# Projection matmuls whose moving columns alternate between the two 256-column halves of a weight row

## Chip, cores and metric

The kernel runs on one core of a Trainium2 chip. The metric is device time in microseconds (us) of one execution. The kernel before takes 1576.56 us, the median of three runs (1575.62 to 1576.97).

## What is computed

One block of a streaming encoder over 256 tokens of width 2048, all in float32:

```
h      = rms_norm(x, g_mix)
proj   = h @ w_in                      # retention q,k,v,gate; attention q,k,v
ret    = silu(gate) * group_norm(retention(q, k, v))
att    = sliding_window_attention_with_sinks(q, k, v)
merged = sigmoid(h @ w_gate_r) * (ret @ w_ret) + sigmoid(h @ w_gate_a) * (att @ w_att)
x      = x + merged @ w_out
x      = x + square(relu(rms_norm(x, g_ffn) @ w_up)) @ w_down      # width 8192
out    = rms_norm(x, g_fin)
```

## The kernel before

**Blocks.** All products with a weight matrix ("projections") are cut into 69 blocks of 2048 weight rows by 512 columns. A block is 16 chunks `k` of 128 rows, two chunks making a unit `u`. Two token tiles `t` of 128 tokens each have a PSUM accumulator of one bank, 512 float32 columns, so one block fills `acc[parity]`, a tile of 128 x 2 x 512; two of these alternate from block to block.

**Three products for one.** Weights come by DMA as float32 into `raw`. ScalarE copies each unit into `whi` as fp32r (the reduced form in which TensorE multiplies in one pass), VectorE subtracts to get the rest, `wlo`; of the activations there are such pairs too (`ta_hi`, `ta_lo`; `tb_`, `tc_`). A projection is hi x hi + hi x lo + lo x hi. So each chunk and token tile takes three matmuls (line 413): the stationary operand is 128 x 128 of the activations, which gives tokens as the output's partitions, and the moving operand is the chunk's 512 weight columns, neighbours in SBUF. The weight split (ScalarE, line 648; VectorE, line 967) uses a ring of eight chunks, and so is paced by the matmuls that release its slots. From block 37 on (the MLP), a quarter of each block's low parts, `low`, comes through a copy on ScalarE (line 656) and an accumulating DMA (line 1402) instead.

**Exceptions.** The first unit of the first block is done with plain float32 operands (line 469), which the program issues as two instructions per product. The last block does one token tile after the other (line 626, `gemm_by_tile`), so that the first tile's end work lies under the second tile's matmuls.

**Order.** The order is written out by hand and kept by semaphores. Stage 1 projects attention q and retention q, k alternately and mixes attention's small matmuls in between (`tail_a`, `tail_r`); stage 2 does attention's gate and branch; stage 3 retention's v and gate, with the retention itself; stage 4 retention's gate and branch and the merging; stage 5 the output projection (four blocks); stage 6 the MLP in four rounds of four `w_up` and four `w_down` blocks.

**Who reads the accumulators.** ScalarE: `scaled` (line 662) for most blocks, and lines 768 and 771, which sort the columns of the first block, keys and values of four heads. VectorE: `rotate` (lines 1094 to 1097, four products with cosines and sines over both token tiles), `gated_attention` (line 1187), the gating in `tail3` (line 1222), `merge` (line 1274), `add_residual` (line 1303), and line 1384 for the last block. A block's accumulator is needed again only by the second block after it. The readers of accumulators stand among the weight splits in the in-order queues of the two engines.

Of the kernel before, what the change touches and what calls it, by code (L numbers as in the profile page):

```python
# [29 lines left out]
P = 128  # L30
D = 2048
S = 256
TILES = S // P
COLS = 512
# [13 lines left out]
ATT_D = 64  # L48
# [75 lines left out]
ACT_COLS, DVE_COLS = 768, 640  # L124
WARM_UP = 10

OWN_STAGE1, OWN_STAGE2, OWN_STAGE3, OWN_STAGE4 = 18, 1, 1, 1

def build(nc, x, x_t, w_in, w_ret, w_att, w_gate, w_out, w_up, w_down, g_fin,  # L130
# [3 lines left out]
    ds = bass.ds  # L134

    ctx = ExitStack()
    with ctx:
# [139 lines left out]
        gained = buf[2][:, 1, :].rearrange("p (k n) -> p k n", n=S)  # L277
        gmix_at = slice(SMALL - 4 * KCH, SMALL - 3 * KCH)

        block = ctx.enter_context(nc.Block())  # L280

# [109 lines left out]
        def _(pe):  # L392
            def gemm(B, hi, lo, u0, u1):

                for u in range(u0, u1):
                    if u == 0 and B.reused:
                        pe.wait_ge(evacuated[B.parity], B.turn)
                    halves = B.very_first and u == 1
                    by_dma = B.ffn and u >= DVE_UNITS
                    if by_dma:  # L400
                        pe.wait_ge(low_full, B.before * 16 + 32)
                        pe.wait_ge(hi_ready, B.part(u))
                    elif not halves:
                        pe.wait_ge(lo_ready, B.low(u))
                    for kk in range(UCH):
                        if halves:
                            pe.wait_ge(half_lo, kk + 1)
                        k, slot = u * UCH + kk, (u * UCH + kk) % (KCH // 2)
                        low = low4[:, k - DVE_UNITS * UCH, :] if by_dma else wlo[:, slot, :]
                        for t in range(TILES):  # L410
                            tok = slice(t * P, (t + 1) * P)
                            for n, (a, b) in enumerate(((hi, whi[:, slot, :]), (hi, low), (lo, whi[:, slot, :]))):
                                last = nc.tensor.matmul(acc[B.parity][:, t, :], a[:, k, tok], b,  # L413
                                                        start=(k == 0 and n == 0), stop=(k == KCH - 1 and n == 2))
                    last.then_inc(unit_done, 1)

# [48 lines left out]
            for k in range(UCH):  # L465
                pe.wait_ge((first_full, second_full)[k], 16)
                pe.wait_ge(xt_gained, k + 1)
                for t in range(TILES):
                    last = nc.tensor.matmul(acc[0][:, t, :], gained[:, k, t * P:(t + 1) * P], raw[:, k, :],
                                            start=(k == 0), stop=False)  # L470
            last.then_inc(unit_done, 1)
            for u in range(1, UNITS):
# [141 lines left out]
            def gemm_by_tile(B):  # L614

                pe.wait_ge(evacuated[B.parity], B.turn)
                for t in range(TILES):
                    tok = slice(t * P, (t + 1) * P)
                    for u in range(UNITS):
                        if t == 0:  # L620
                            pe.wait_ge(lo_ready, B.low(u))
                        for kk in range(UCH):
                            k = u * UCH + kk
                            whi_k, wlo_k = [last_slot(part, u)[:, kk, :] for part in range(2)]
                            for n, (a, b) in enumerate(((tb_hi, whi_k), (tb_hi, wlo_k), (tb_lo, whi_k))):
                                done = nc.tensor.matmul(acc[B.parity][:, t, :], a[:, k, tok], b,
                                                        start=(k == 0 and n == 0), stop=(k == KCH - 1 and n == 2))
                    done.then_inc(tile_done, 1)

# [7 lines left out]
        def _(act):  # L637
# [20 lines left out]
            def scaled(B, dst, func, scale):  # L658

                act.wait_ge(unit_done, B.unit(UNITS - 1))  # L660
                for t in range(TILES):
                    last = nc.scalar.activation(dst[:, t, :], acc[B.parity][:, t, :], func, scale=scale[:, t:t + 1])
                return last

            def hi_from_turned(turn, dst, g):
# [84 lines left out]
            def stage1(j, first):  # L750
                A, R = Block(B1, 2, j), Block(B1 + 1, 2, j)
                if first:
# [9 lines left out]
                    act.wait_ge(unit_done, Block(0).unit(UNITS - 1))  # L762
                    kd = buf[1][:].rearrange("p t (g e d) -> p t g e d", e=2, d=ATT_D)
                    vd = vwin[:].rearrange("p w g (e d) -> p w g e d", e=2)
                    kv = [acc[0][:, t, :].rearrange("p (s g d) -> p s g d", s=2, d=ATT_D) for t in range(TILES)]
                    twice = [(t, e) for t in range(TILES) for e in range(2)]
                    for t, e in twice:
                        last = nc.scalar.activation(kd[:, t, :, e, :], kv[t][:, 0], ACT.Copy, scale=rstd[:, t:t + 1])
# [189 lines left out]
        def _(dve):  # L958
# [125 lines left out]
            def rotate(g, B):  # L1084

                dve.wait_ge(unit_done, B.unit(UNITS - 1))
                half = RET_QK // 2
                v = acc[B.parity][:].rearrange("p t (h x d) -> p t h x d", x=2, d=half)
                cos = roper[:, 0].unsqueeze(2).to_broadcast([P, TILES, 4, half])
                sin = roper[:, 1].unsqueeze(2).to_broadcast([P, TILES, 4, half])  # L1090
                o = buf[1][:].rearrange("p t (h x d) -> p t h x d", x=2, d=half)
                tmp = [b[:].rearrange("p t (h d) -> p t h d", d=half)[:, :, 4 * i:4 * i + 4, :]
                       for b in (buf[2], buf[3]) for i in range(2)]
                V_.tensor_tensor(tmp[0], v[:, :, :, 0, :], cos, ALU.mult)
                V_.tensor_tensor(tmp[1], v[:, :, :, 1, :], sin, ALU.mult)
                mine.step(V_.tensor_tensor(tmp[2], v[:, :, :, 1, :], cos, ALU.mult))
                V_.tensor_tensor(tmp[3], v[:, :, :, 0, :], sin, ALU.mult).then_inc(evacuated[B.parity], 1)
                dve.wait_ge(turned_1, g + T_Q)
                dve.wait_ge(evacuated[B.parity], B.turn + 1)
                V_.tensor_tensor(o[:, :, :, 0, :], tmp[0], tmp[1], ALU.subtract)  # L1100
                V_.tensor_tensor(o[:, :, :, 1, :], tmp[2], tmp[3], ALU.add).then_inc(rope_ready, 1)
# [80 lines left out]
            def gated_attention(j):  # L1182
# [1 line left out]
                B = Block(B2 + 1, 2, j)  # L1184
                dve.wait_ge(unit_done, B.unit(UNITS - 1))
                mine.wait(dve)
                V_.tensor_tensor(mix[:, :, ds(j * COLS, COLS)], buf[2][:], acc[0][:], ALU.mult).then_inc(evacuated[0], 1)

            tail_a(3, Block(B2), Block(B2 - 1))
            tail_r(3, Block(B2 + 1))  # L1190
# [15 lines left out]
            def tail3(j, B):  # L1206
# [12 lines left out]

                dve.wait_ge(rgate_ready, j + 1)  # L1220
                dve.wait_ge(ret_read, j + 1)
                V_.tensor_tensor(buf[3][:], buf[1][:], acc[0][:], ALU.mult).then_inc(evacuated[0], 1)
                dve.wait_ge(evacuated[0], Block(B3 + 1, 2, j).turn + 1)
                V_.scalar_tensor_tensor(buf[3][:].rearrange(flat), buf[2][:].rearrange(flat), 1.0,
                                        buf[3][:].rearrange(flat), ALU.add, ALU.mult).then_inc(gated_ready, 1)
# [42 lines left out]
            def merge(j):  # L1268
# [2 lines left out]
                dve.wait_ge(unit_done, B.unit(UNITS - 1))  # L1271
                mine.wait(dve)
                dve.wait_ge(t_full, j + T_STAGE4)
                V_.tensor_tensor(buf[3][:], buf[2][:], acc[0][:], ALU.mult).then_inc(evacuated[0], 1)
                dve.wait_ge(evacuated[0], B.turn + 1)
                V_.tensor_tensor(buf[3][:], buf[3][:], mix[:, :, ds(j * COLS, COLS)], ALU.add).then_inc(m_ready, 1)

# [22 lines left out]
            def add_residual(B, j):  # L1300
                dve.wait_ge(unit_done, B.unit(UNITS - 1))
                sl = mix[:, :, j * COLS:(j + 1) * COLS]
                V_.tensor_tensor(sl, sl, acc[B.parity][:], ALU.add).then_inc(evacuated[B.parity], 1)

            def inverse_rms(done):
                mine.step(V_.tensor_reduce(sum2[:], ssq2[:], AX.X, ALU.add))
# [74 lines left out]
            for t in range(TILES):  # L1381
                sl = mix[:, t, early:D]
                dve.wait_ge(tile_done, t + 1)
                V_.tensor_tensor(sl, sl, acc[0][:, t, :], ALU.add).then_inc(added, 1)
                dve.wait_ge(added, t + 1)
                V_.tensor_tensor(final[:, t, early:D], sl, gfin[:, early:D], ALU.mult).then_inc(final_g, 1)
                dve.wait_ge(last_sq, t + 1)
# [89 lines left out]
```

## Time and profile before

| | before |
|---|---|
| median of three runs | 1576.56 us |
| the profiled execution | 1575.47 us |
| its span, first to last instruction | 1573.5 us |
| TensorE matmul busy | 1562.0 us, 99% |
| TensorE weight load busy | 1280.2 us, 81% |
| VectorE busy | 1023.7 us, 65% |
| ScalarE busy | 795.1 us, 51% |
| DMA, mean | 212 GB/s |
| granted TensorE clock, mean | 0.999 of full |

Busy time counts each instruction from start to modelled end, and matmuls overlap: one that lasts 389 ns is followed by the next after some 227 ns. The rate of the stream is therefore read from start times, or from the chain of waits, which gives a stretch of the array's work with its count.

### The profile page before, as it was taken

How to read it: one execution, taken by the hardware profiler on the slowest of the kernel's cores; microseconds unless marked ns; L12 is line 12 of the kernel's file. 1: busy time of each engine (PE TensorE's matmuls, PEld its weight loads, DVE VectorE, ACT ScalarE, POOL GpSimd, SP SyncE). 2: the span in 40 equal slices, each digit the busy share in tenths (PEclk: the TensorE clock that was granted, in tenths of full speed). 3: DMA queues.
4: the chain of work that ended last, by engine and by line, in shares of the span. 5: the costliest groups of instructions: out<-in, count | busy, mean ns of one | idle time of the engine just before them, and what ended most of it. 6: DMA issues, size and time to landing. Idle time of an engine off the chain costs nothing.

```text
span 1573.5 us, 18925 instructions
## 1 busy us (share of the span) xinstructions
PE 1562.0 (99%) x7008; PEld 1280.2 (81%) x7008; DVE 1023.7 (65%) x1344; ACT 795.1 (51%) x1023; POOL 39.4 (3%) x52
## 2 busy tenths in 40 slices
PE   9999999999999999999999999999999999999998
PEld 7777777888888888888878888888888888888886
DVE  5977876544456777666689877347753576437744
ACT  6555555443444444444444555555554555555553
POOL 0000000000000000000000000000000000000000
PEclk9999999999999999999999999999999999999999
DMA  9644554556655565565565877888778887888873
GB/s 362 206 144 152 183 160 161 187 187 222 208 171 175 188 201 168 180 206 192 203 231 181 260 237 237 253 230 254 233 236 251 240 249 218 252 240 241 249 222 117
DMA packets 154392, 333.93 MB, mean 212 GB/s; under 512 B 5600, under 2 KB 5728, under 8 KB 149856
## 3 DMA queue, kind: packets, MB, share of 16 engines
q1 hardware_dynamic: 149296, 299.61, 56.3%
q0 software_dynamic: 4464, 32.51, 10.9%
q10 hardware_dynamic: 576, 1.06, 0.2%
q8 instruction: 36, 0.59, 0.2%
q14 instruction: 20, 0.16, 0.0%
HBM read 298.55 MB, written 2.10 MB: 191 GB/s over the span
## 4 chain that ended last, share of the span: by engine, by line
PE 92%; DVE 4%; DMA 2%; issue 1%; ACT 1%; SPq 0%; POOL 0%; POOLq 0%; DVEq 0%
PE acc L413 89%; DMA raw<-in_w_in 2%; DVE wlo L967 1%; DVE buf L976 1%; PE tps L428 1%; PE pps L455 1%; PE pps L438 0%; DVE kT L976 0%; DVE qT L976 0%; PE sps L446 0%; DVE ta_lo L1366 0%; ACT whi L648 0%; PE tps L557 0%; PE tps L556 0%; PE tps L558 0%
## 5 line engine op out<-in xcount | busy, mean ns | idle before, releaser
L648 ACT ACTIVATE whi<-raw 128x1024 fp32r<-128x1024 f32 x542 | 572.4, 1059 | 662.3 <-PE acc L413 658.2
L967 DVE TENSOR_TENSOR wlo<-raw,whi 128x1024 fp32r<-128x1024 f32 x480 | 586.0, 1226 | 460.9 <-ACT whi L648 457.7
L413 PE MATMUL acc<-whi,ta_hi 128*128 128x512 f32 x1308 | 514.4, 393 | 0.8 <-DVE ta_lo L1010 0.4
L413 PE MATMUL acc<-whi,ta_lo 128*128 128x512 f32 x1308 | 509.5, 390 | 0.0
L413 PE MATMUL acc<-wlo,ta_hi 128*128 128x512 f32 x1180 | 459.2, 389 | 0.0
L413 PEld LDWEIGHTS acc<-whi,ta_hi 128*128 128x128 f32 x1308 | 245.5, 188 | 57.9 <-issue 4.2
L413 PEld LDWEIGHTS acc<-whi,ta_lo 128*128 128x128 f32 x1308 | 245.5, 188 | 51.8
L413 PE MATMUL acc<-whi,tb_hi 128*128 128x512 f32 x736 | 286.7, 389 | 0.0
L413 PE MATMUL acc<-whi,tb_lo 128*128 128x512 f32 x736 | 286.3, 389 | 0.0
L413 PEld LDWEIGHTS acc<-wlo,ta_hi 128*128 128x128 f32 x1180 | 221.6, 188 | 44.8
L413 PE MATMUL acc<-wlo,tb_hi 128*128 128x512 f32 x616 | 239.6, 389 | 0.0
L976 DVE STREAM_TRANSPOSE buf<-buf 32x256 f32<-32x256 f32 x384 | 167.4, 436 | 6.8
L413 PEld LDWEIGHTS acc<-whi,tb_hi 128*128 128x128 f32 x736 | 138.2, 188 | 29.3 <-issue 0.8
L413 PEld LDWEIGHTS acc<-whi,tb_lo 128*128 128x128 f32 x736 | 138.2, 188 | 28.8
L413 PEld LDWEIGHTS acc<-wlo,tb_hi 128*128 128x128 f32 x616 | 115.6, 188 | 23.8
L656 ACT ACTIVATE low<-raw 128x2048 fp32r<-128x2048 f32 x31 | 59.1, 1906 | 0.0
L413 PE MATMUL acc<-whi,tc_hi 128*128 128x512 f32 x128 | 50.0, 390 | 0.9 <-DVE wlo L967 0.9
L413 PE MATMUL acc<-whi,tc_lo 128*128 128x512 f32 x128 | 49.8, 389 | 0.0
L413 PE MATMUL acc<-low,ta_hi 128*128 128x512 f32 x128 | 49.8, 389 | 0.0
L413 PE MATMUL acc<-wlo,tc_hi 128*128 128x512 f32 x128 | 49.8, 389 | 0.0
L1402 POOL DMA_DIRECT2D low<-raw x31 | 27.0, 870 | 889.8 <-ACT low L656 889.8
L413 PE MATMUL acc<-low,tb_hi 128*128 128x512 f32 x120 | 46.7, 389 | 0.0
(139 smaller groups left out, 789.4 us busy)
## 6 DMA issues: line engine op xcount, KB each, us to landing
raw<-in_w_in SPq DMA_DIRECT2D x66, 1024.0 KB, 5.2
raw<-in_w_up SPq DMA_DIRECT2D x64, 1024.0 KB, 5.5
raw<-in_w_down SPq DMA_DIRECT2D x64, 1024.0 KB, 5.2
raw<-in_w_gate SPq DMA_DIRECT2D x32, 1024.0 KB, 5.3
low<-raw POOLq DMA_DIRECT2D x31, 1024.0 KB, 8.1
raw<-in_w_att SPq DMA_DIRECT2D x16, 1024.0 KB, 5.0
raw<-in_w_ret SPq DMA_DIRECT2D x16, 1024.0 KB, 5.0
raw<-in_w_out SPq DMA_DIRECT2D x16, 1024.0 KB, 5.1
```

The lines of the kernel that those rows point to most:

```text
L413: last = nc.tensor.matmul(acc[B.parity][:, t, :], a[:, k, tok], b, start=(k == 0 and n == 0), stop=(k == KCH - 1 and n == 2))
L428: last = nc.tensor.matmul(score[:, h, m, 0:kn], qT[part, c, 2 * m:2 * m + 2, :].rearrange("p a n -> p (a n)"), keys[part, k0:k0 + kn], sta ...
L455: last = nc.tensor.matmul(pps[part, 2 * h:2 * h + 2, :].rearrange(flat), vst[:, KEYS[c][2], part], probT[:, 2 * h:2 * h + 2, :].rearrange( ...
L648: nc.scalar.activation(whi[:, s:s + UCH, :], raw[:, u * UCH:(u + 1) * UCH, :], ACT.Copy).then_inc(hi_ready, 1)
L656: nc.scalar.activation(low4[:], raw[:, DVE_UNITS * UCH:KCH, :], ACT.Copy, scale=-1.0).then_inc(low_set, 1)
L967: V_.tensor_tensor(wlo[:, s:s + UCH, :], raw[:, u * UCH:(u + 1) * UCH, :], whi[:, s:s + UCH, :].bitcast(f32), ALU.subtract).then_inc(lo_re ...
L976: last = V_.transpose(dst(i, o), src[i:i + SQ, :, :, o:o + SQ])
L1402: pool.dma_start(low4[:].bitcast(f32), raw[:, DVE_UNITS * UCH:KCH, :], accum_op=ALU.add).then_inc(low_full, 16)
```

## The change

In SBUF nothing moves. A matmul's moving operand, 512 neighbouring columns, is read through a view that gives column 0, 256, 1, 257, ..., 255, 511. The output is written to neighbouring addresses of the bank, so bank position 2n holds column n, and position 2n+1 column 256+n. All readers of the accumulators read with a step of two elements to get the old order back; what they write lies as before. This holds for lines 413, 469 and 626 alike. Matmuls of attention and retention, the transposes, weight loads and DMAs are as they were.

`rotate` is cut by token tile, since its view would have a dimension too many: eight multiplications over 128 x 256 elements stand for four over 128 x 512, and one counted step on VectorE's own semaphore goes away (OWN_STAGE1 is 17 for 18). The counting of all other semaphores stays.

```diff
-OWN_STAGE1, OWN_STAGE2, OWN_STAGE3, OWN_STAGE4 = 18, 1, 1, 1
+OWN_STAGE1, OWN_STAGE2, OWN_STAGE3, OWN_STAGE4 = 17, 1, 1, 1
...
+        def halves_in_turn(cols):
+            return cols.rearrange("p (b n) -> p n b", b=2)
+        def paired(bank):
+            return bank.rearrange("p (n b) -> p n b", b=2)
+        def unpaired(bank):
+            return bank.rearrange("p (n b) -> p b n", b=2)
+        def unpaired_tiles(banks):
+            return banks.rearrange("p t (n b) -> p t b n", b=2)
+        def by_half(cols):
+            return cols.rearrange("p (b n) -> p b n", b=2)
+        def by_half_tiles(cols):
+            return cols.rearrange("p t (b n) -> p t b n", b=2)
...
-                                last = nc.tensor.matmul(acc[B.parity][:, t, :], a[:, k, tok], b,
+                                last = nc.tensor.matmul(paired(acc[B.parity][:, t, :]), a[:, k, tok], halves_in_turn(b),
...
-                    last = nc.tensor.matmul(acc[0][:, t, :], gained[:, k, t * P:(t + 1) * P], raw[:, k, :],
+                    last = nc.tensor.matmul(paired(acc[0][:, t, :]), gained[:, k, t * P:(t + 1) * P], halves_in_turn(raw[:, k, :]),
...
-                                done = nc.tensor.matmul(acc[B.parity][:, t, :], a[:, k, tok], b,
+                                done = nc.tensor.matmul(paired(acc[B.parity][:, t, :]), a[:, k, tok], halves_in_turn(b),
...
-                    last = nc.scalar.activation(dst[:, t, :], acc[B.parity][:, t, :], func, scale=scale[:, t:t + 1])
+                    last = nc.scalar.activation(by_half(dst[:, t, :]), unpaired(acc[B.parity][:, t, :]), func, scale=scale[:, t:t + 1])
...
-                    kv = [acc[0][:, t, :].rearrange("p (s g d) -> p s g d", s=2, d=ATT_D) for t in range(TILES)]
+                    kv = [acc[0][:, t, :].rearrange("p (g d s) -> p s g d", s=2, d=ATT_D) for t in range(TILES)]
...
-                v = acc[B.parity][:].rearrange("p t (h x d) -> p t h x d", x=2, d=half)
...
+                v = acc[B.parity][:].rearrange("p t (h x d b) -> p t x b h d", x=2, d=half, b=2)
...
-                V_.tensor_tensor(tmp[0], v[:, :, :, 0, :], cos, ALU.mult)
-                V_.tensor_tensor(tmp[1], v[:, :, :, 1, :], sin, ALU.mult)
-                mine.step(V_.tensor_tensor(tmp[2], v[:, :, :, 1, :], cos, ALU.mult))
-                V_.tensor_tensor(tmp[3], v[:, :, :, 0, :], sin, ALU.mult).then_inc(evacuated[B.parity], 1)
+                for t in range(TILES):
+                    part = [a[:, t].rearrange("p (b h) d -> p b h d", b=2) for a in tmp]
+                    V_.tensor_tensor(part[0], v[:, t, 0], cos[t], ALU.mult)
+                    V_.tensor_tensor(part[1], v[:, t, 1], sin[t], ALU.mult)
+                    V_.tensor_tensor(part[2], v[:, t, 1], cos[t], ALU.mult)
+                    last = V_.tensor_tensor(part[3], v[:, t, 0], sin[t], ALU.mult)
+                last.then_inc(evacuated[B.parity], 1)
...
-                V_.tensor_tensor(buf[3][:], buf[2][:], acc[0][:], ALU.mult).then_inc(evacuated[0], 1)
+                V_.tensor_tensor(by_half_tiles(buf[3][:]), by_half_tiles(buf[2][:]), unpaired_tiles(acc[0][:]),
+                                 ALU.mult).then_inc(evacuated[0], 1)
...
-                V_.tensor_tensor(sl, sl, acc[B.parity][:], ALU.add).then_inc(evacuated[B.parity], 1)
+                V_.tensor_tensor(by_half_tiles(sl), by_half_tiles(sl), unpaired_tiles(acc[B.parity][:]),
+                                 ALU.add).then_inc(evacuated[B.parity], 1)
...
-                V_.tensor_tensor(sl, sl, acc[0][:, t, :], ALU.add).then_inc(added, 1)
+                V_.tensor_tensor(by_half(sl), by_half(sl), unpaired(acc[0][:, t, :]), ALU.add).then_inc(added, 1)
```

Lines 1187 and 1222 are changed in the manner of line 1274.

## Rows read from the trace of the kernel before

**Rows 1.** The page: shares of the span, and the granted clock in 40 slices.

```profile
PE 1562.0 (99%) x7008; PEld 1280.2 (81%) x7008; DVE 1023.7 (65%) x1344; ACT 795.1 (51%) x1023; POOL 39.4 (3%) x52
PEclk9999999999999999999999999999999999999999
```

**Rows 2.** Chain of waits in order of time: start us, us, what.

```profile
274.40 168.87 PE acc L413 x744
...
451.88 0.91 PE acc L413 x4
452.79 0.43 PE tps L556 x2
```

**Rows 3.** Timeline of the last block, three starts: start us, us, engine, line, instruction.

```profile
1558.11 0.39 PE L626 MATMUL acc<-whi,tb_lo 128*128 128x512 f32 x1
...
1565.36 0.39 PE L626 MATMUL acc<-ta_lo,tb_hi 128*128 128x512 f32 x1
...
1565.59 0.39 PE L626 MATMUL acc<-ta_hi,tb_lo 128*128 128x512 f32 x1
```

**Rows 4.** Windows: PE, PEld, DVE, ACT, POOL busy (instructions), clock, DMA share, GB/s.

```profile
5.50:9.30 3.80, 3.80 (x10) 1.54 (x9) 1.73 (x4) 2.42 (x6) 0.00 (x0) 1.00 1.03 361
300.00:440.00 140.00, 140.00 (x620) 115.95 (x619) 68.76 (x58) 59.48 (x61) 0.00 (x0) 1.00 0.63 206
1558.00:1565.00 7.00, 7.00 (x33) 5.79 (x32) 1.01 (x2) 0.94 (x1) 0.13 (x1) 1.00 0.39 150
```

**Rows 5.** What the tensor engine waited for, all of it.

```profile
PE acc L413 <- DVE wlo L967: 1.3, 2, 0.9
PE tps L428 <- DVE qT L976: 1.2, 1, 1.2
PE pps L463 <- DVE mix L1019: 1.1, 1, 1.1
PE acc L413 <- DVE ta_lo L1010: 0.4, 1, 0.4
```

**Rows 6.** Timeline, weight loads of the float32 passes over 512 columns (line 469).

```profile
6.17 0.19 PEld L469 LDWEIGHTS acc<-raw,buf 128*128 128x128 f32 x1 [0.24 <-issue]
...
8.31 0.19 PEld L469 LDWEIGHTS acc<-raw,buf 128*128 128x128 f32 x1 [0.24 <-issue]
```

**Rows 7.** Matmuls by form: count | busy us, mean ns of one | idle before.

```profile
L413 PE MATMUL acc<-whi,ta_lo 128*128 128x512 f32 x1308 | 509.5, 390 | 0.0
L413 PEld LDWEIGHTS acc<-whi,ta_lo 128*128 128x128 f32 x1308 | 245.5, 188 | 51.8
L556 PE MATMUL tps<-buf,ptr 128*128 128x256 f32 x16 | 4.8, 378 | 0.0
```

**Rows 8.** Accumulator readers: count, duration ns min/median/max, first and last start us.

```profile
L1303 DVE TENSOR_TENSOR mix<-mix,acc x19: 1212/1214/1217, 805.5 to 1551.0; 128x1024 f32<-128x1024 f32 x19
L1094 DVE TENSOR_TENSOR buf<-acc,roper x4: 683/692/692, 78.3 to 236.7; 128x512 f32<-128x512 f32 x4
L1187 DVE TENSOR_TENSOR mix<-buf,acc x4: 1212/1214/1221, 287.9 to 418.3; 128x1024 f32 x3, 128x1024 f32<-128x1024 f32 x1
L1222 DVE TENSOR_TENSOR buf<-buf,acc x4: 1220/1222/1222, 465.9 to 608.4; 128x1024 f32<-128x1024 f32 x4
L1274 DVE TENSOR_TENSOR buf<-buf,acc x4: 1212/1214/1217, 651.9 to 782.5; 128x1024 f32<-128x1024 f32 x4
L1384 DVE TENSOR_TENSOR mix<-mix,acc x2: 680/684/689, 1555.7 to 1566.0; 128x512 f32<-128x512 f32 x2
...
L662 ACT ACTIVATE buf<-acc,rstd x48: 667/677/691, 52.0 to 1480.5; 128x512 f32<-128x512 f32 x48
L662 ACT ACTIVATE buf<-acc,rstd_half x24: 671/677/691, 265.3 to 760.0; 128x512 f32<-128x512 f32 x24
L768 ACT ACTIVATE buf<-acc,rstd x4: 469/476/481, 38.7 to 39.8; 128x256 f32<-128x256 f32 x4
L771 ACT ACTIVATE vwin<-acc,rstd x4: 490/504/516, 40.2 to 41.2; 128x256 f32<-128x256 f32 x4
```

**Rows 9.** Groups by form, for comparison with rows 8.

```profile
L1338 DVE TENSOR_TENSOR buf<-buf 128x1024 f32<-128x1024 f32 x16 | 19.6, 1226 | 0.0
L1072 DVE TENSOR_TENSOR prob<-prob,rden 128x256 f32<-128x256 f32 x4 | 1.7, 425 | 0.1
```

More of the change, by code:

```diff
@@ L1087, in rotate @@
                 half = RET_QK // 2
-                v = acc[B.parity][:].rearrange("p t (h x d) -> p t h x d", x=2, d=half)
-                cos = roper[:, 0].unsqueeze(2).to_broadcast([P, TILES, 4, half])
-                sin = roper[:, 1].unsqueeze(2).to_broadcast([P, TILES, 4, half])
+                v = acc[B.parity][:].rearrange("p t (h x d b) -> p t x b h d", x=2, d=half, b=2)
+                cos, sin = [[roper[:, a, t].unsqueeze(1).unsqueeze(2).to_broadcast([P, 2, 2, half]) for t in range(TILES)]
+                            for a in range(2)]
                 o = buf[1][:].rearrange("p t (h x d) -> p t h x d", x=2, d=half)
@@ L1186, in gated_attention @@
                 mine.wait(dve)
-                V_.tensor_tensor(mix[:, :, ds(j * COLS, COLS)], buf[2][:], acc[0][:], ALU.mult).then_inc(evacuated[0], 1)
+                V_.tensor_tensor(by_half_tiles(mix[:, :, ds(j * COLS, COLS)]), by_half_tiles(buf[2][:]), unpaired_tiles(acc[0][:]),
+                                 ALU.mult).then_inc(evacuated[0], 1)
             tail_a(3, Block(B2), Block(B2 - 1))
@@ L1221, in tail3 @@
                 dve.wait_ge(ret_read, j + 1)
-                V_.tensor_tensor(buf[3][:], buf[1][:], acc[0][:], ALU.mult).then_inc(evacuated[0], 1)
+                V_.tensor_tensor(by_half_tiles(buf[3][:]), by_half_tiles(buf[1][:]), unpaired_tiles(acc[0][:]),
+                                 ALU.mult).then_inc(evacuated[0], 1)
                 dve.wait_ge(evacuated[0], Block(B3 + 1, 2, j).turn + 1)
@@ L1273, in merge @@
                 dve.wait_ge(t_full, j + T_STAGE4)
-                V_.tensor_tensor(buf[3][:], buf[2][:], acc[0][:], ALU.mult).then_inc(evacuated[0], 1)
+                V_.tensor_tensor(by_half_tiles(buf[3][:]), by_half_tiles(buf[2][:]), unpaired_tiles(acc[0][:]),
+                                 ALU.mult).then_inc(evacuated[0], 1)
                 dve.wait_ge(evacuated[0], B.turn + 1)
```

## The prediction

> **What bounds the kernel.** I read the page's shares first: TensorE is busy 99% of the span at full clock in every slice, VectorE 65%, ScalarE 51% [rows 1]. The waits of the array confirm it: the four entries come to 4.0 us [rows 5]. Nothing but the length of the matmul stream matters, so the next question is what one matmul costs, and that is not its 389 ns but the distance of starts. The chain shows 744 projection matmuls in 168.87 us, 0.2270 us each, and the last block, where VectorE and ScalarE are almost idle, shows 33 intervals from 1558.11 to 1565.59, 7.48 us, 0.2267 us each [rows 2 to 4]. I take 0.2268. It doesn't depend on what the other engines do.
>
> How many there are follows from the code: 67 blocks of 96 (16 chunks, 2 tiles, 3 products), 84 of the first block's units 1 to 7, and 96 of the last: 6612. At 0.2268 us they make 1499.6 us, 95% of the span.
>
> **What 0.2268 us consists of.** At full clock, 2.4 GHz, 512 columns at one per cycle are 0.2133 us. The plain float32 passes are the measure: 256 columns take 0.43 us for two passes, 0.215 each [rows 2], and 512 columns take (8.31 - 6.17)/5 = 0.428 us per pass [rows 6], both two cycles a column and both with a weight load of their own. So a pass with the same 512 cycles costs 0.215 there and 0.2268 here, 0.0118 more. The single durations agree, 378 against 390 ns [rows 7]. The weight load, 188 ns, fits under either. 
>
> **The change, part by part.**
>
> *Moving order.* 6612 matmuls have no two successive columns beside each other any more; they lie 1 KB apart. No row has such a moving operand, so I bound its price. Below: the surcharge of 0.0118 goes, a gain. Nothing excludes it. Above: one column at a time is served at a quarter of today's rate, twice the 0.428 of the float32 pass, 0.856. Between them lies 0.428 itself, the only slower rate of a 512-column stream that the trace has [rows 6]. I take it: if one fetch serves two neighbours now, it serves one after the change, and the stream runs at two cycles a column. The surcharge does not come on top, since the float32 pass has none. Price: 6612 x (0.428 - 0.2268) = 6612 x 0.2012 = +1330.3 us.
>
> The Trainium skill has a rule against this change (SBUF — State Buffer, section "Door 1: The DMA port swizzle"): SBUF is read in lines of 16 bytes, and at least two consecutive accesses must hit a line to reach full bandwidth. By it neighbouring float32 columns hit a line four times, and alternating ones once. It states no size for the penalty, and no row here shows one.
>
> *The float32 unit.* Eight passes of line 469 at 0.428 us [rows 6]; by the same reasoning they already run at the slower rate. 0 us, at most another 8 x 0.428 = 3.4.
>
> *Accumulator readers.* They step by two elements, 8 bytes. No reader in the trace does. Reading an accumulator in order is as fast as reading SBUF: 1214 against 1226 ns for 1024 columns [rows 8, 9], so PSUM isn't the limit of these today. Lower bound 0, upper bound a doubling: 31 instructions of 1.21 to 1.22 us on VectorE, 37.7 us in all, and 72 of 0.677 us, 48.7 us, on ScalarE. These engines have 35% and 49% of the span free, and a block's readers have until the second block after it, some 21.8 us (96 x 0.2268). That cover would only go if the split of weights fell behind, and it waits for the array. On the path to the end stand five places: lines 768 and 771 (1.9 and 2.0 us for four each), which feed the first attention group on which the array waits 1.2 us [rows 5, 8], the last merge (1.21), the last residual add of stage 5 (1.21), and line 1384 after the last matmul (0.68). Doubled they give 7.0 us; I take 1 us, near the lower end, since the nearest row says that PSUM keeps up.
>
> The Trainium skill (Advanced Engine Details and Errata, section "PSUM Cachelines") gives PSUM lines of 8 bytes, two float32, and says that every two consecutive elements should be contiguous. The change keeps the array's writes so and breaks only the readers' order, for which the rule would favour the 7.0 over the 1.
>
> *rotate.* Four multiplications of 0.68 to 0.69 us become eight of some 0.425 [rows 8, 9]: 3.40 for 2.75, +0.65 us, four times, alongside matmuls. Its cover is VectorE's slack. 0 us. The counted step that goes away was waited for by nobody at once.
>
> *What the slower stream gives back.* The array's waits for VectorE in mid-kernel, 1.3 + 1.2 + 0.4 = 2.9 us [rows 5], vanish, since both other engines get twice the time. -2.9 us. The end work after the last matmul stays.
>
> **Sum.** 1573.5 + 1330.3 + 1.0 - 2.9 = 2901.9 us of span. The profiled execution lasts 1575.47, 1.97 more than its span, and the median is 1.09 above it: 2905 us. For this case alone I allow 0.427 without slack to 0.454 (the stretch doubled too): 2895 to 3075 us.
>
> **The rivals.**
>
> *B, the order costs nothing.* The moving read may keep both streams at hand, and the surcharge may belong to fp32r itself. Then only the readers count: 1576.6 + 0 to 7.0, about 1577.6 us. For: no row shows any dependence of the matmul rate on addresses. Against: the stretch of 0.0118 that only the fastest stream has. Chance 0.19, of which 0.04 lies above 1579.7.
>
> *C, a partial cost.* One stall of a quarter cycle per column, 640 cycles, 0.267 us: 6612 x (0.267 - 0.2268) = +266, 1843 us. It stands for anything well between B and the forecast. Chance 0.10.
>
> *D, a quarter of the rate.* If the fetch of neighbours is what sets 0.2268 today, with four columns to a fetch, then single columns need four times as many. At 0.856: 6612 x 0.6292 = +4160, 5735 us. For: it explains why the fp32r stream is stretched and the float32 one, at half its rate, isn't. Against: it asks that today's stream is exactly at the limit. The 16-byte line of the Trainium skill's SBUF page is four float32, which favours it. Chance 0.20, and 0.06 for other prices between the forecast and D.
>
> *E, faster.* The surcharge comes from neighbours that collide, and reading two distant places in turn avoids it. It lies in every one of the 6612 matmuls, and it pays as soon as it exceeds the readers' cost, 0.15 ns a matmul at my 1 us. In full: 6612 x 0.0118 = -78, 1499 us. For: the surcharge is there, the weight load isn't its cause, and the float32 passes avoid it by being slow. Against: alternation makes more fetches, not fewer. Chance 0.12.
>
> **How the numbers follow.** The forecast has 0.33, more than any other case, and is the predicted time. The rivals lie far apart, so 8 in 10 need a wide range: with B, C, D and what is between it holds 0.88, and leaving out B or D would leave out more than 2 in 10. It runs from 1574 to 5740. About 0.2%, 3.2 us, can be told from no change here. Faster is E, 0.12; same is B without its upper part, 0.15; slower is the rest, 0.04 + 0.10 + 0.33 + 0.06 + 0.20 = 0.73.
>
> **What would show it.** The distance of matmul starts in a stretch like 300 to 440 us decides: 0.428 for the forecast, 0.227 for B, 0.856 for D, 0.215 for E. By the forecast the mean duration of a line 413 matmul grows from 390 to about 590 ns, the weight loads stay at 188, their busy share falls to near 44%, VectorE falls to some 36%, and the granted clock stays full. Should the clock fall to its lower level, the rate is that of the clock and not of the fetch, and my step is wrong even if the time fits. The readers' rows say whether a step of two costs: 1214 and 677 ns if not. The forecast is wrong if the start distance isn't within 0.42 to 0.46 us.

## The result, and the profile after

The changed kernel takes 1514.22 us, median of four runs (1512.37 to 1514.65), against 1576.46 us: ratio 0.9602, 95% interval 0.959 to 0.9614. It is 62.2 us faster where I forecast 1330 us slower. That is rival E, to which I gave 0.12, with 62 of its 78 us.

The page of the changed kernel, shares of the span and granted clock, beside [rows 1]:

```profile
span 1512.1 us, 18941 instructions
PE 1494.5 (99%) x7008; PEld 1288.6 (85%) x7008; DVE 1022.6 (68%) x1360; ACT 791.3 (52%) x1023; POOL 39.4 (3%) x52
PEclk9999999999999999999999999999999999999999
```

The array is still what bounds the kernel, at a mean granted clock of 0.998, and its busy time has become 67.5 us shorter. The chain of waits says by how much per matmul, beside [rows 2]:

```profile
268.90 160.78 PE acc L437 x744
```

The same 744 matmuls take 160.78 us, 216.1 ns each, where they took 168.87, 227.0 ns: 10.9 ns less. The groups by form agree: the single matmul lasts 380 ns for 390, no gap has closed (line 437 is line 413 of before), and that the weight load is as it was, beside [rows 7]:

```profile
L437 PE MATMUL acc<-whi,ta_lo 128*128 128x512 f32 x1308 | 496.5, 380 | 0.0
L437 PEld LDWEIGHTS acc<-whi,ta_lo 128*128 128x128 f32 x1308 | 247.5, 189 | 35.2
```

The plain float32 passes went the other way. The timeline of weight loads shows their starts 0.54 us apart, (9.18 - 6.48)/5, for 0.428 in [rows 6]:

```profile
6.48 0.19 PEld L493 LDWEIGHTS acc<-raw,buf 128*128 128x128 f32 x1 [0.34 <-issue]
...
9.18 0.19 PEld L493 LDWEIGHTS acc<-raw,buf 128*128 128x128 f32 x1 [0.35 <-issue]
```

The readers of the accumulators take what they took [rows 8], with their step of two; only `rotate`, cut in eight, takes 8 x 0.417 us for four of 0.68 to 0.69:

```profile
L1333 DVE TENSOR_TENSOR mix<-mix,acc x19: 1214/1214/1217, 775.7 to 1490.7; 128x1024 f32<-128x1024 f32 x19
L1120 DVE TENSOR_TENSOR buf<-acc,roper x8: 415/417/426, 80.3 to 234.1; 128x256 f32<-128x256 f32 x8
...
L686 ACT ACTIVATE buf<-acc,rstd x48: 667/677/687, 51.9 to 1422.9; 128x512 f32<-128x512 f32 x48
```

And the array waits more than in [rows 5], 9.7 us in all for 4.0. Some of the entries:

```profile
PE acc L437 <- DVE wlo L991: 4.4, 9, 1.6
PE tps L452 <- DVE qT L1000: 1.8, 1, 1.8
...
PE acc L437 <- DMA low<-raw: 0.7, 1, 0.7
```

6612 matmuls at 10.87 ns less are 71.9 us. The span fell by 61.4. So two questions were open: why does this order of the columns make the matmul cheaper, and where did 10.5 us go?

### The profile page after: what moved, and what is told of

It is laid out like the page before. It is cut to its first block, busy times and chain, and to the rows that moved or that the text cites. A ratio compares the mean times of both kernels' runs of the same rounds, so it can differ in the third digit from the quotient of the medians.

```text
span 1512.1 us, 18941 instructions
## 1 busy us (share of the span) xinstructions
PE 1494.5 (99%) x7008; PEld 1288.6 (85%) x7008; DVE 1022.6 (68%) x1360; ACT 791.3 (52%) x1023; POOL 39.4 (3%) x52
## 4 chain that ended last, share of the span: by engine, by line
PE 81%; DVE 11%; issue 2%; ACT 2%; DMA 2%; SPq 0%; POOL 0%; DVEq 0%; POOLq 0%; ACTq 0%
PE acc L437 78%; DVE buf L1000 4%; DVE wlo L991 3%; DMA raw<-in_w_in 2%; ACT whi L672 1%; DVE qT L1000 1%; DMA low<-raw 1%; PE tps L452 1%; PE pps L479 1%; PE pps L462 0%; DVE kT L1000 0%; DVE mix L1333 0%; DVE tb_lo L1039 0%; DVE buf L1369 0%; ACT prob L705 0%
## 5 line engine op out<-in xcount | busy, mean ns | idle before, releaser
L437 PE MATMUL acc<-whi,ta_hi 128*128 128x512 f32 x1308 | 501.9, 384 | 3.1 <-DVE wlo L991 1.9
L437 PE MATMUL acc<-whi,ta_lo 128*128 128x512 f32 x1308 | 496.5, 380 | 0.0
L437 PE MATMUL acc<-wlo,ta_hi 128*128 128x512 f32 x1180 | 447.8, 380 | 0.0
L437 PE MATMUL acc<-whi,tb_hi 128*128 128x512 f32 x736 | 279.6, 380 | 0.8 <-DVE tb_lo L1039 0.6
L437 PE MATMUL acc<-whi,tb_lo 128*128 128x512 f32 x736 | 278.9, 379 | 0.0
L437 PEld LDWEIGHTS acc<-wlo,ta_hi 128*128 128x128 f32 x1180 | 223.5, 189 | 31.1 <-issue 0.3
L437 PE MATMUL acc<-wlo,tb_hi 128*128 128x512 f32 x616 | 233.5, 379 | 0.0
```

The source lines that it names most:

```text
L437: last = nc.tensor.matmul(paired(acc[B.parity][:, t, :]), a[:, k, tok], halves_in_turn(b), start=(k == 0 and n == 0), stop=(k == KCH - 1 a ...
```

## Experiments on the matmul

**A row of matmuls (m1).** A small program loads 4096 weight columns and 2048 activation columns, converts them, and issues groups of 48 matmuls (24 for float32, two passes each), with `WR` fp32r, `WB` bf16, `W` float32 for the moving columns. Every order writes the bank in order, unless said otherwise. Two of its lines, with the names of banks shortened:

```
for i in range(48): mm(bank(i), fr(i), WR[:, c(i):c(i) + 512])                                   # in order
for i in range(48): mm(paired(bank(i)), fr(i), WR[:, c(i):c(i) + 512].rearrange("p (b n) -> p n b", b=2))   # halves in turn
```

> Not the reference's computation: 28 groups of 24 or 48 back-to-back matmuls, each with its own order of the moving columns or kind of operand; all else is left out and the output is filler. Read: distance of starts per group. From the whole kernels: fp32r in order 226.8 ns, halves in turn about 216. Theory 1 (neighbours fetched back to back stall now and then, two distant places in turn avoid it): halves, quarters, eighths and 128 parts in turn all near 216; two blocks of 2, whose columns 0, 2, 1, 3 stay in the same 16 bytes, remain at 226; steps of 2 and more near 216; pairs in turn (0, 1, 256, 257) between. Theory 2 (the weight load's reads collide with the moving read): with half the weight columns (64) the in-order surcharge falls from 11 to some 5 ns. Theory 3 (the view's two dimensions matter, not the distance): every group with a two-dimensional view is at 216, the steps of 2, 4 and 8 stay at 226. Theory 4 (a start-up cost per matmul): 384 columns in order carry the same 11 ns as 512; by theory 1 three quarters, 8 ns. bf16 in order, half the bytes: 216 by theory 1, 227 if width doesn't matter. Plain float32: in order 428 a pass, halves in turn 540 as in the changed kernel's first unit; whether 0, 2, 1, 3 costs the same tells whether distance matters there.

The chain of waits of this program, one row per group, gives the distance of starts as length over count:

```profile
32.40 10.88 PE ps L99 x48
43.27 10.36 PE ps L100 x48
53.63 13.59 PE ps L101 x48
...
112.76 10.95 PE ps L104 x48
123.70 10.36 PE ps L105 x48
...
185.86 16.32 PE ps L111 x48
202.18 21.81 PE ps L112 x48
...
277.85 8.33 PE ps L116 x48
286.18 7.80 PE ps L117 x48
293.98 11.04 PE ps L118 x48
305.02 10.36 PE ps L119 x48
...
336.67 23.25 PE ps L122 x48
359.92 20.60 PE ps L123 x48
380.52 25.92 PE ps L124 x48
```

| order of the moving columns (fp32r unless said) | line | ns per matmul |
|---|---|---|
| in order | 99 | 226.7 |
| halves in turn: 0, 256, 1, 257 | 100 | 215.8 |
| quarters in turn | 101 | 283.1 |
| eighths in turn | 102 | 487 |
| 128 parts in turn | 103 | 461 |
| in order, start 1 to 3 columns off | 115 | 229 |
| 0, 2, 1, 3, 4, 6, 5, 7 | 104 | 228.1 |
| 0, 4, 1, 5, 2, 6, 3, 7 (blocks of 4 in turn) | 105 | 215.8 |
| blocks of 8 to 128 in turn | 106 to 110 | 215.8 |
| pairs in turn: 0, 1, 256, 257 | 111 | 340 |
| step of 2; of 4; of 8 | 112; 113; 114 | 454; 461; 431 |
| 384 columns in order; halves in turn | 116; 117 | 173.5; 162.5 |
| 64 weight columns, in order; halves in turn | 118; 119 | 230; 215.8 |
| bf16, halves in turn | 122 | 484 |
| float32, a pass, in order; halves in turn | 123; 124 | 429; 540 |

The granted clock is 1.00 in every one of these groups. The whole kernels' two numbers are here with VectorE and ScalarE at rest and next to no DMA, so they don't need the other engines' traffic. Theory 2 (weight load) is out: with half the weight columns the surcharge doesn't shrink, it is 14 ns. Theory 3 (shape of the view) is out: 0, 2, 1, 3 has the same kind of view and no gain. Theory 1 holds for the distance of 16 bytes between 0, 2, 1, 3 and 0, 4, 1, 5, but fails for quarters, eighths, 128 parts and steps, all of which it put near 216, and for pairs, which it put between the two rates. Theory 4 holds: 384 columns carry 11.0 ns, as 512 do.

**A second row (m2)**, to tell two sharper theories apart. Halves in turn, each with a step, and blocks of 4 that start off the 16-byte border:

```
for i in range(48): mm(paired(bank(i)), fr(i), WR[:, 0:1024].rearrange("p (b n e) -> p n b e", b=2, e=2)[:, :, :, i % 2])
for i in range(48): mm(dealt(bank(i)), fr(i), WR[:, 2:514].rearrange("p (m b n) -> p m n b", b=2, n=4))
```

> Again only a row of groups of matmuls, output filler. Theory P (two readers): the array takes fp32r columns in pairs, the even positions of the order through one reader and the odd ones through another; a reader that gets four successive accesses in one 16-byte stretch runs free (215.8 ns), with two it pays a fixed start-up (226.8), with one it halves (454). Theory Q (distance only: any two places 16 bytes or more apart in turn are free). Halves in turn, each read with a step of 2: P 227, Q 216. With a step of 4: P some 460, Q below 300. Halves in turn starting 1 to 3 columns off: both 216 (P allows 229). Blocks of 4 in turn, start shifted by 2: P 227, Q 216. Size of the surcharge (in order less in turn): 11 at 320 and 448 columns if it is per matmul, 7 and 10 if per column. In order and in turn mixed one by one: 221 if each matmul pays for its own start. In order with a jump in the middle, or without accumulation: 227. bf16 (in order 216): step 2 by P free or at 227, in blocks of 2, 4 and 8 in turn slower than in order if four neighbours are a fetch; pairs and fours in turn tell how wide it is; stepped writes of the bank 216 if the array's writes don't care. Plain float32: pairs in turn and steps of 2 near 429 or, as with halves, 540.

The chain of waits again:

```profile
52.22 10.73 PE ps L101 x48
62.94 7.04 PE ps L102 x48
69.98 6.52 PE ps L103 x48
76.50 9.73 PE ps L104 x48
86.23 9.08 PE ps L105 x48
95.31 10.88 PE ps L106 x48
106.20 21.75 PE ps L107 x48
127.95 10.42 PE ps L108 x48
138.37 10.89 PE ps L109 x48
...
260.42 20.38 PE ps L119 x47
280.79 21.76 PE ps L120 x48
...
324.15 43.21 PE ps L122 x48
```

Halves with a step of 2 (line 106) take 226.7 ns, with a step of 4 (107) 453, and shifted blocks of 4 (109) 226.9. These are the three places where P and Q part, and P has all three; Q has none. Halves that start 1 to 3 columns off (108) take 217.1, which P left open. The surcharge is 10.8 at 320 columns (102, 103), 13.5 at 448 (104, 105), 11 at 384 and 512: it doesn't grow with the columns, and why 448 stands out is open. Mixed one by one (101) it is 223.5, more than the 221 for half of it. An order with a jump and one without accumulation were at 227.5 and 226.7.

P reads the fp32r rows so: the order's even positions go through one reader, the odd ones through another. In order, each gets 0, 2, 4, 6: two accesses in 16 bytes, and the surcharge. 0, 2, 1, 3 gives two as well. Halves in turn and blocks of 4 give each reader 0, 1, 2, 3: four, and no surcharge. Steps of 2, 4 and 8 and the 128 parts give each one access in 16 bytes, and about half the rate (431 to 461).

P does not fit every row. With quarters (283) and with pairs in turn (340) each reader alternates between two places, one access in 16 bytes at a time, which by P's own words is half the rate; both are faster. Eighths (487) are slower than half. So P is a picture that fits the orders with one place per reader, and is not shown: no run looks into the readers, and why two accesses cost a fixed 11 ns is not explained. What is shown is the rate of each order.

Other types differ. bf16 in order takes 216; blocks of 2 and of 4 in turn take 215.8, blocks of 8, which are 16 bytes apart, 485, pairs in turn 271, a step of 2 226. Writing the bank with a step of two doubles bf16, 429 ns (line 119: 20.60 us from its first start to that of line 120, over 48), and leaves float32 at 429 a pass, as in order. Pairs in turn and a step of 2 cost a float32 pass 453 and 450, a step of 4 900 (lines 120 to 122). Stepped writes of fp32r were not tried.

**In the kernel.** Four versions of the kernel before, each with one other moving order in lines 413, 469 and 626, and all readers as before (so that columns come out permuted):

```diff
-                                last = nc.tensor.matmul(acc[B.parity][:, t, :], a[:, k, tok], b,
+                                last = nc.tensor.matmul(OUT(acc[B.parity][:, t, :]), a[:, k, tok], IN(b),
```

with IN "p (b n) -> p n b" for b=2 (r1) and b=4 (r3), "p (m b n) -> p m n b" with b=2 for n=2 (r2) and n=4 (r4), and OUT the one that writes neighbours.

> The kernel before with the new moving order alone: all readers of the accumulators stay as they were, so that columns come out permuted (the restoring of the order is left out), and rotate keeps its four products. If the stepped readers of the changed kernel cost nothing, as their durations of 1214 and 677 ns say: 1514 us, within 1 us of the changed kernel. If they cost on the path what the prediction's 1 us or more took: 1507 to 1513 us.

1514.23 us (1512.15 to 1514.43), the changed kernel's time. So the moving order alone makes the gain, and the stepped readers and the cut `rotate` cost nothing that can be told in the whole.

> The kernel before with the moving order 0, 2, 1, 3, 4, 6, 5, 7 ... (the same kind of view, but never more than 16 bytes apart), readers as before, columns permuted. From the row of matmuls, 228.1 ns each: 1576.5 + 6612 x 0.0014 = 1586 us, slower than before. If it were the view's shape, or any order but the plain one, that gains: 1514 us.

1576.68 us, ratio 0.9998 (0.9989 to 1.0008): no change, where I expected 1586. I had gone by the 228.1 of the row of matmuls; here the chain shows 744 in 168.87 us, the 227.0 of the order 0, 1, 2, 3:

```profile
274.56 168.87 PE acc L419 x744
```

Why the row had 1 ns more is open. The theory that any order but the plain one gains is out all the same.

> The kernel before with the moving order 0, 4, 1, 5, 2, 6, 3, 7, 8, 12 ... (16 bytes apart), readers as before, columns permuted. From the row of matmuls, 215.8 ns as for halves: 1514 us. If the kernel's gain needed the distance of 1 KB (another bank of the memory, less in the way of VectorE, ScalarE and DMA): 1540 us or more.

1512.82 us (1512.56 to 1513.82), and 744 matmuls in 160.78 us, to the digit what halves give:

```profile
268.58 160.78 PE acc L419 x744
```

16 bytes of distance do what 1 KB does. The float32 passes are 0.54 us apart here too.

> The kernel before with the moving columns taken from the four 128-column quarters in turn, readers as before, columns permuted. From the row of matmuls, 283.1 ns each: 1576.5 + 6612 x 0.0563 = 1949 us, less 3 us of waits that vanish. It tells whether the rate of the row of matmuls carries over where it is a loss, and so whether this one number decides. A rival: within the kernel, ScalarE and VectorE on the same memory make it worse still, above 2000 us.

1901.37 us in its one run, 45 us less than expected. Its chain has a stretch of 744 matmuls in 210.96 us, 283.5 ns as in the row of matmuls, but one of 4164 in 1138.15 us, 273.3 ns; that difference alone is 42 us. In stage 3 the two rates alternate from one stretch of 156 matmuls to the next (44.17, 42.64, 44.17 us), with small matmuls between, so the 283 of the row holds for part of the kernel only, and I can't explain the second value. The rival is out: ScalarE and VectorE make nothing worse.

**The float32 unit put back (v1).**

```diff
-                    last = nc.tensor.matmul(paired(acc[0][:, t, :]), gained[:, k, t * P:(t + 1) * P], halves_in_turn(raw[:, k, :]),
+                    last = nc.tensor.matmul(unpaired(acc[0][:, t, :]), gained[:, k, t * P:(t + 1) * P], by_half(raw[:, k, :]),
```

> The changed kernel with one part undone: the eight float32 passes of the first unit take their moving columns in order again, and write the bank with a step of two, so that columns still lie where the later matmuls put them. In the changed kernel their starts are 0.54 us apart, in the kernel before 0.428. If the price is that of the moving read: 0.428 again, 8 x 0.112 = 0.9 us earlier at the end of the unit, and 0 to 0.9 us in the end (1513.3 to 1514.2 us). If the stepped writes cost as much as the order saves (the rival): 0.54 or more, no gain.

The starts are 0.43 us apart again (six from 6.19 to 8.34), and the whole takes 1513.85 us (1512.3 to 1514.41), which these runs can't tell from 1514.22. So the 0.54 is the price of the moving order, and stepped writes cost the float32 pass nothing.

## Experiments on the missing 10 us

Where it went can be read by comparing the times of the same event in both chains:

| event | before | after | gained so far | matmuls' share up to here, about |
|---|---|---|---|---|
| first attention scores | 65.87 | 66.57 | -0.7 | 2.6 |
| start of the stretch of 744 | 274.40 | 268.90 | 5.5 | 10.8 |
| start of the stretch of 804 | 597.94 | 577.37 | 20.6 | 25.6 |
| last split before stage 5's chain | 780.26 | 750.94 | 29.3 | 34.3 |
| first matmuls of the MLP | 885.36 | 854.10 | 31.3 | 39.3 |
| last accumulator read | 1566.0 | 1504.7 | 61.3 | 71.9 |

The share is 10.87 ns times the projection matmuls up to the event (240, 996, 2352, 3156, 3612 and 6612). From 274 us to the entry of stage 5 nothing is lost (23.8 gained, 23.5 due). The start loses 3.3 us, stage 1 2.0, stage 5 3.0, and the MLP with the last block 2.6.

**The start (v3), beside the changed kernel again (a0).** v3 is v1 with two copies moved from VectorE to ScalarE:

```diff
+                    act.wait_ge(evacuated[0], 1)
+                    nc.scalar.activation(vwin[0:64, 1], vwin[64:128, 0], ACT.Copy)
+                    nc.scalar.activation(vwin[64:128, 1], vwin[0:64, 2], ACT.Copy).then_inc(vshift, 1)
...
-                    V_.tensor_copy(vwin[0:64, 1], vwin[64:128, 0])
-                    V_.tensor_copy(vwin[64:128, 1], vwin[0:64, 2]).then_inc(vshift, 1)
```

> The changed kernel itself, for a comparison on the same chip with the next one: 1514.2 us, 1512.3 to 1514.7.

1513.83 us (1512.59 to 1514.22).

> The changed kernel with the float32 unit in order (its starts 0.43 us apart for 0.54) and, in stage 1, the two copies within vwin (0.42 us each) moved from VectorE to ScalarE, behind the split of the block's last units. Theory: about 11 us of the matmuls' gain are given back, the largest piece where VectorE is busy without a gap from 40 to 67 us and the array waits for it, 1.8 us before the first attention scores alone, after which the granted clock drops for a while (0.88 from 60 to 70 us). If so, 0.84 us less on VectorE end that wait 0.8 us earlier, and the whole is 1511 to 1513.4 us, 0.8 us or more below the changed kernel. If the loss lies elsewhere or ScalarE's two copies come in the way: no difference.

1513.28 us (1511.84 to 1514.06): no difference to be told, and the scores start at 66.43 for 66.59. The chain of waits of v3 says why:

```profile
39.87 1.20 ACT buf L792 x3
41.06 1.47 ACT vwin L795 x4
42.53 0.95 ACT whi L672
...
43.58 1.23 DVE wlo L994
```

Without the copies VectorE isn't earlier, since ScalarE's eight scaled copies and the next split end at 43.48; the copies on VectorE had lain beside them. The start is a chain from the DMA through both engines that no matmul is in, and a faster array only waits for it longer. My theory, that these two copies on VectorE hold it up, fell; the rest of VectorE's work there was not relieved.

**VectorE's load later on (v4, v5).** In stages 4 to 6 half of the transposes are left out, once in the changed kernel and once in the one before:

```diff
-                for i, o in pieces[n0:n1]:
+                for i, o in pieces[n0:n1:every]:
...
-                    turn(by_chunk(src), to_tokens(turned), at[0], at[1], t_full if u == u1 - 1 else None)
+                    turn(by_chunk(src), to_tokens(turned), at[0], at[1], t_full if u == u1 - 1 else None, 2)
```

> The changed kernel with half of the 32x32 transposes left out wherever a block's result is turned in stages 4 to 6 (24 turns, 8 transposes of 0.436 us each less, 84 us of VectorE in all; the turned tiles keep old data there). Theory: from 750 us on the array waits 4.7 us in the changed kernel and 1.3 us in the kernel before, because the faster stream catches up with VectorE at the turns. Then with the turns halved most of the 4.7 go: 1509 to 1511.5 us, 3 us or more below the changed kernel. Rival: these waits come from the chain of dependent steps (ScalarE's copies, the DMA that subtracts), not from VectorE's load: less than 1 us.

1506.15 us (1505.46 to 1507.5), 7.7 below a0 and below my range of 1509 to 1511.5.

> The kernel before with the same transposes left out. It waits only 1.3 us from 780 us on, so at most that is to be had: 1575 to 1576.5 us. If it gains as much as the changed kernel does, VectorE's load held both back alike and explains nothing of the missing 10 us.

1574.84 us against 1576.87, ratio 0.9985 (0.9976 to 0.9995): 2.0 us, just beyond my range. So the turns hold the changed kernel back by some 6 us more than the kernel before, about what stage 5, the MLP and the last block lose in the table.

**Amount or order of work? (v6, v7).** In stage 5 of the changed kernel the stretches of 36 matmuls recur every 21.3 us, where 96 matmuls take 20.7 (96 x 0.2158):

```profile
786.72 8.05 PE acc L437 x36
794.79 1.06 ACT whi L672
...
797.02 1.23 DVE mix L1333
...
801.86 1.23 DVE wlo L991
...
806.74 1.24 DVE wlo L991
808.02 8.05 PE acc L437 x36
```

v6 takes work off VectorE there; v7 leaves the work and moves it. Both have v1's float32 unit. The first diff is v6's on ScalarE (VectorE does the gain for the last group only), the second v7's:

```diff
+                    if j < GROUPS:
+                        act.wait_ge(t_full, T_STAGE5 + j)
+                        for i in range(GCH):
+                            k = (j - 1) * GCH + i
+                            last = nc.scalar.activation(buf[2][:].rearrange("p t (k n) -> p (t k) n", n=S)[:, i, :],
+                                                        turned[:, i, :], ACT.Copy, scale=gffn[:, k:k + 1])
+                        last.then_inc(t_free, 1)
```

```diff
-                    split_and_turn(B, 4, 6, T_STAGE5 + j - 1, mix[:, :, (j - 1) * COLS:j * COLS],
+                    last_turn = 7 if j < GROUPS else 6
+                    split_and_turn(B, 4, last_turn, T_STAGE5 + j - 1, mix[:, :, (j - 1) * COLS:j * COLS],
...
-                    split(B, 6, 7)
+                    split(B, last_turn, last_turn + 1)
```

In v7 ScalarE's split of unit 7 also moves ahead of its copy of the activations.

> The changed kernel with the float32 unit in order, and with the multiplication by the norm's gain (1.15 us on VectorE) done by ScalarE, as four scaled copies of 128 x 256, for three of the four column groups of stage 5. Theory: in stage 5 the changed kernel's blocks start 21.3 us apart, which is VectorE's work of one block, while 96 matmuls at 215.8 ns need 20.7; the kernel before needs 21.8 for them and hid VectorE. If so, the three blocks that are relieved come down to 20.7 us, 0.6 us each, and the whole is about 1.8 us faster: 1511.5 to 1512.8 us. If the distance is set by the chain through ScalarE instead, the longer way by it keeps 21.3 us or makes it worse, and the whole is at 1514 us or above.

1512.84 us (1511.96 to 1514.16). The time lies at the edge of what I expected, and for another reason: the stretches start at 764.80, 786.10, 807.40 and 828.70, still 21.3 us apart. So it isn't the sum of VectorE's work in a block that sets the pace, and the gain, 1.15 us, isn't on the path that does. The transposes of v4 are.

> The changed kernel with the float32 unit in order, and in stage 5, for three of the column groups, the sixteen transposes spread before the weight splits of units 4, 5 and 6 instead of 4 and 5 (so ten stand before unit 5's split, not sixteen); no work is added or left out. Theory: the 21.3 us between blocks of stage 5 are a closed loop: 36 matmuls of units 5 to 7 (8.05 us), ScalarE's copy 1.07, split 1.23, residual add 1.23, sixteen transposes 7.1, two splits 2.46, and then unit 5's matmuls again; the array's own 20.7 us are less. Six transposes fewer in the loop are 2.6 us, so the array sets the pace there again: blocks 20.7 us apart for these three, 1.8 us in all, 1511.5 to 1512.6 us. Rival: another loop (through unit 6 or 7, or the low parts of the activations) closes at the same length, and nothing changes.

1511.0 us (1510.15 to 1512.2), the fastest version with the reference's computation; its runs lie below all of a0's, though on another chip. The loop no longer sets the pace, and the array runs through 324 matmuls:

```profile
763.08 70.21 PE acc L437 x324
833.32 1.06 ACT whi L672
...
835.55 1.23 DVE mix L1334
```

From the start of the stretch of 804 to the first matmuls of the MLP v7 takes 275.0 us (575.03 to 850.04) and the changed kernel 276.7 (577.37 to 854.10): 1.7 us, for the 1.8 that I expected of the three blocks. Another part of its 2.8 us against a0 is the clock. In the profiled run of the changed kernel the granted clock dropped after the long waits of the start, in v7's it didn't. Windows, and the first 36 matmuls between the attention scores, of the changed kernel, then of v7:

```profile
60.00:70.00 10.00, 8.24 (x39) 6.65 (x38) 9.63 (x19) 3.23 (x6) 0.00 (x0) 0.88 0.50 164
...
67.23 9.65 PE acc L437 x36
```

```profile
60.00:70.00 10.00, 8.24 (x44) 6.91 (x43) 9.66 (x18) 3.22 (x10) 0.00 (x0) 1.00 0.47 144
...
66.57 7.97 PE acc L437 x36
```

The same 36 matmuls take 1.7 us more at the dropped clock, which is most of the 2.0 that stage 1 loses in the table. The array waits before them in v7 as well (8.24 us busy of 10 in both windows), so the wait alone doesn't decide it. In the kernel before no window after the start, and before the end work, shows less than 1.00. The runs of one version spread over 2 us, those of the changed kernel from 1512.4 to 1514.7; that the clock falls in some and not in others may be why. In v7 the three runs with a mean clock of 0.999 take 1510.2 to 1511.0 us, the two with 0.997 and 0.998 take 1511.7 and 1512.2, which fits but was not tested.

## Why the prediction was wrong

**The step that failed** is the price of the moving order: "if one fetch serves two neighbours now, it serves one after the change, and the stream runs at two cycles a column". It measured -10.9 ns a matmul instead of +201.2. I had bounded it by -11.8 and taken the middle, because 0.428 us was the only slower rate in the trace. But that rate belongs to float32 passes, which take 429 ns in order where fp32r and bf16 take 227 and 216 for as many columns, and says nothing on fetches. It was not even a rate that a change of order leaves alone, as I held: those passes went from 0.428 to 0.540 us. A rate seen for another kind of operand isn't a price for this one.

**The reading was right up to there.** The number of matmuls, their 0.2268 us, the independence of the other engines, and the surcharge of 0.0118 over a pass with the same 512 cycles all stood, and the last was the clue: a cost that in the trace the fastest stream alone has, and that the weight load doesn't explain (that speed isn't the reason either, bf16 shows, as fast and without it, 216). Rival E took it at face value; I weighed it down with "alternation makes more fetches, not fewer". The runs show that it is no loss if a column's neighbour doesn't come next; by picture P, which isn't shown, what counts is whether the columns two, four and six places later lie in the same 16 bytes. E's own reason, neighbours that collide, isn't shown either: in the order 0, 2, 1, 3, 4, 6, 5, 7 only every other step goes to a neighbour, and the surcharge stays whole (227.0). So E's price came true, and why the surcharge goes remains open below the level of the order.

**The rules of the Trainium skill.** The 16-byte line of the Trainium skill's page SBUF — State Buffer, section "Door 1: The DMA port swizzle", shows in the rows: the gain appears when the two places are 16 bytes apart, 0, 4, 1, 5, and not at 0, 2, 1, 3, and a step of 4 halves the rate of fp32r and of float32 (461 for 227, 900 for 429). Its condition, two consecutive accesses to a line, is met by fp32r with a step of 2, at 454, and broken by halves in turn, at 215.8. So by that rule the change had to lose, and the measurement decides against it for fp32r; for bf16 (484 for 216) and float32 (540 for 429) it agrees. The PSUM line of the Trainium skill's Advanced Engine Details and Errata, section "PSUM Cachelines", agrees for bf16's stepped writes, 429 for 216, and not for a float32 pass, 429 for 429, nor for the readers: VectorE and ScalarE read with a step of 8 bytes at 1214 and 677 ns, as before.

**Readers.** I took 1 us of 0 to 7.0; it was 0. **The float32 unit.** I took 0, at most 3.4; it was 8 x 0.112 = 0.9 us at its place, of which nothing can be told in the whole (v1). **rotate.** 8 x 0.417 = 3.3 us, beside matmuls, as forecast.

**What the stream gives back** had the wrong sign for the case that came true. I wrote it for a slower stream, and costed rival E "In full: 6612 x 0.0118 = -78" with nothing given back. Measured: 71.9 us of matmul time and 61.4 of span. Of the 10.5 between them, 5.7 are waits (9.7 us for 4.0), 0.9 the float32 passes and 1.7 the clock; some 2 us are not accounted for.

**The range** of 1574 to 5740 missed 1514 although it was wide, since I had let it end at "no effect", with the surcharge lying open as a gain of known size. One term of rival D was also misread: 0.856 us is a quarter of the full rate of one column a cycle; a quarter of today's 0.2268 would be 0.907. Nothing else hangs on it.

## What to carry to other kernels

For fp32r matmuls with 512 moving columns, take the columns alternately from two places at least 16 bytes apart, each read in order from a 16-byte border, and write the bank in order (no other way of writing was tried): 215.8 ns for 226.7. Off the border the gain shrinks (halves, 217.1) or goes (blocks of 4, 226.9). Not for bf16 or float32, not from four places, and not in pairs or with steps. When a kernel is 99% bound by one engine, a gain on it can bring back closed loops, chains of work through the other engines that end where they begin, that were hidden by one or two per cent. Look for stretches that recur at the same distance. Taking work away outside the loop did not shorten it (v6); taking work out of the loop by a change of order did (v7).

## What the runs showed of the hardware that I had not expected

- The rate of fp32r matmuls depends on the order of the moving columns: 215.8, 226.7, 283, 340, 454 ns for the same 512 columns, with only the order changed.
- The surcharge of the plain order is about 11 ns a matmul at 320, 384 and 512 columns (13.5 at 448), so shorter matmuls pay more of it in proportion (7% of the plain order's time at 320 columns, 5% at 512).
- Halves in turn more than double bf16, 484 ns for 216, and slow float32 by a quarter, 540 for 429 a pass, while they speed fp32r up.
- A bank written with a step of two doubles a bf16 matmul and leaves a float32 pass alone; VectorE and ScalarE read such a bank at full speed.
